# A two-layer decoder trunk with gathered expert rows: six row buffers and eleven held chunks in place of seven and ten, pooling moved to VectorE

## The chip, the core and the metric

One core of one Trainium2 chip. The metric is the device time of one execution, in microseconds (us); the kernel before takes 1603.8 us (median of 3 runs, 1603.68 to 1604.42). All arithmetic is float32.

## What is computed

The input x is 256 tokens by 1024 channels; each of two layers does this to it:

```python
h = rmsnorm(x, g_mix)
p, q, k, v, gl = split(h @ w_in)             # 512, 512, 512, 512 and 2048 columns
a = (trailing_mean(p, windows 2/4/8/16 on 4 groups of 128 channels) - p) @ w_pool * pool_scale
b = causal_attention(q, k, v, 8 heads, ALiBi) @ w_attn_up
x = x + (sigmoid(gl[:, :1024]) * a + sigmoid(gl[:, 1024:]) * b) @ w_out
xt = rmsnorm(x, g_ffn)
# per token and head (8 heads): two 128-key score lists, top 16 of each, top 16 of the 256 sums,
# softmax -> 16 experts out of 16384, each one row u of w_peer_u and one row v of w_peer_v
x = x + sum_over_128_experts(prob * gelu(u . xt) * v)
```

and a last rmsnorm ends it. With 256 tokens the attention is plain causal attention.

## The kernel before, in words

**Windows.** The work is cut into four windows (w = 0 to 3): layer 0 tile 0, layer 0 tile 1, layer 1 tile 0, layer 1 tile 1; a tile is 128 tokens, one on each partition. A window has a *stream* and a *mix*. The stream gathers the 128 expert rows of each token of the tile: gather g (0 to 511) is one indirect DMA from GpSimd's queue (line 1182) that brings, for each of 128 tokens, one u row and one v row, 8 KB per partition and 1 MB in all, into one of RING = 7 ring buffers. The mix is all that precedes it for the tile: norm, projections, attention, pooling, gates, the two output projections, and the queries and key searches that give the experts.

**Ticks.** The stream of a window runs over 64 ticks of two rows (r = 0 and 1). Except for window 0, whose mix runs first, the mix of window w runs inside the stream of window w - 1. Each engine's program is written out by `streamed` (line 311): the rows in order, and the pieces of the mixes between them wherever a generator's `yield when(w, tick)` says. `when` adds `TICKS * (w - 1) + MIX_START`, so with MIX_START = 4 a piece at 31 stands in tick 35 of the window before. Waits on an engine hold up all that stands behind them on it.

**One row.** VectorE multiplies the u half by the token and sums (`dot`, line 1051); ScalarE makes the gelu weight of it in five small operations (lines 789 to 797). Then the v half is added with that weight: on TensorE, after ScalarE writes the weight on a diagonal (line 807), by products with the diagonal that pile up in two PSUM banks, `ybank` (line 622, four instructions per row); or on VectorE straight into x (`weighted`, line 1064, one instruction, at the start of the next tick). `takes_chunk` (line 282) holds the ticks at which a weight chunk is due, and there row r = 0 goes to VectorE and only r = 1 to TensorE. GpSimd issues gather g when row g - 7 was added (it waits on pe_summed or dve_summed); it issues in order.

**Boundary of windows.** In `hand_over` (line 1037) VectorE writes the new tile's tokens with the gain that TensorE spread over the partitions (`everywhere`, line 352, at tick 58 of the mix); `close` (line 1067) waits until both engines have added all rows of the old window and adds ybank to x (line 1072), and TensorE waits for that before its first row of the new window (line 612). In the last window TensorE first loads x into ybank (line 616).

**Weights.** The weights of a layer are 30 chunks of 1 MB (w_in 0 to 15, attention up 16 and 17, w_out 18 to 21, queries 22 to 29), due at CHUNK_TICKS. Chunks 16 to 25 are *held* in SBUF for both tiles of a layer (HELD = 10), so the second tile does not load them again; the others pass through W_SLOTS = 2 slots, each refilled when its chunk was used. In window 0 the first 16 chunks pass through RING - 1 ring buffers, as the ring is idle then. SyncE's queue issues all chunk loads in order (line 1207), with `heads` (line 1209), which reloads keys and gains for layer 1 once the last query score of window 1's mix is computed.

**Pooling.** p comes out with tokens on partitions (`rows_by`, line 405) and is multiplied on TensorE by banded 128 x 128 matrices from `constants` (lines 496 to 514); for tile 0 a further product gives `carry`, what its last 16 tokens add to tile 1. ScalarE copies carry and the result mT to SBUF (lines 712 and 713).

## Time and profile before

| | |
|---|---|
| median of 3 runs | 1603.8 us |
| the profiled execution | 1599.52 us, span 1597.7 us |
| TensorE matmul busy | 84% of the span |
| VectorE, ScalarE, GpSimd busy | 69%, 58%, 41% |
| moved by DMA | 647.49 MB, mean 405 GB/s |
| row gathers | 512 of 1 MB |
| chunk loads | 100 of 1 MB (64 to the slots, 20 to held buffers, 16 to the ring) |
| granted TensorE clock, mean | 0.952 |

Busy shares are averages over the whole span. In the profile PE is TensorE, PEld its weight load, DVE VectorE, ACT ScalarE, POOL GpSimd and SP SyncE.

### The profile page before, as it was taken

How to read it: one execution, taken by the hardware profiler on the slowest of the kernel's cores; microseconds unless marked ns; L12 is line 12 of the kernel's file. 1: busy time of each engine (PE TensorE's matmuls, PEld its weight loads, DVE VectorE, ACT ScalarE, POOL GpSimd, SP SyncE). 2: the span in 40 equal slices, each digit the busy share in tenths (PEclk: the TensorE clock that was granted, in tenths of full speed). 3: DMA queues.
4: the chain of work that ended last, by engine and by line, in shares of the span. 5: the costliest groups of instructions: out<-in, count | busy, mean ns of one | idle time of the engine just before them, and what ended most of it. 6: DMA issues, size and time to landing. Idle time of an engine off the chain costs nothing.

```text
span 1597.7 us, 18942 instructions
## 1 busy us (share of the span) xinstructions
PE 1346.7 (84%) x5676; PEld 814.6 (51%) x5676; DVE 1097.2 (69%) x2608; ACT 932.2 (58%) x3344; POOL 655.5 (41%) x516
## 2 busy tenths in 40 slices
PE   8998888988987888977898887888988987777876
PEld 7985656644663356643465445655555522223222
DVE  1059978865777877745577797876667876777545
ACT  1226547557756645534775574555676666667766
POOL 0014434355444533323544353334444455455563
PEclk9999999999999999987999899989999999999999
DMA  9939999999999999999999999999999999999996
GB/s 381 391 125 423 422 423 422 424 419 398 413 421 418 410 422 423 422 425 421 392 420 422 392 419 424 423 422 423 397 407 423 421 422 421 421 421 419 415 422 283
DMA packets 90943, 647.49 MB, mean 405 GB/s; under 512 B 10024, under 2 KB 11480, under 8 KB 12504
## 3 DMA queue, kind: packets, MB, share of 16 engines
q0 software_dynamic: 73728, 536.90, 81.3%
q1 hardware_dynamic: 16788, 109.15, 16.5%
q8 instruction: 45, 0.74, 0.2%
q14 instruction: 58, 0.48, 0.1%
q10 hardware_dynamic: 324, 0.23, 0.0%
HBM read 645.19 MB, written 1.05 MB: 404 GB/s over the span
## 4 chain that ended last, share of the span: by engine, by line
DMA 47%; PE 25%; DVE 18%; issue 4%; ACT 4%; POOL 1%; DVEq 0%; ACTq 0%; POOLq 0%
DMA ring<-in_uv,expert 47%; PE ybank L622 12%; DVE ring L1051 7%; PE bank L433 6%; PE bank L571 4%; DVE xs L1064 2%; ACT wgt L797 1%; POOL ring L1182 1%; ACT diag L807 1%; PE bank L413 1%; DVE buf L836 1%; DVE si L842 1%; ACT th L795 1%; DVE ci L842 1%; DVE buf L886 1%
## 5 line engine op out<-in xcount | busy, mean ns | idle before, releaser
L1182 POOL DMA_INDIRECT ring<-in_uv,expert x512 | 655.3, 1280 | 921.6 <-PE ybank L622 584.6
L622 PE MATMUL ybank<-ring,diag 128*128 128x512 f32 x1664 | 836.3, 638 | 214.3 <-ACT diag L807 209.0
L1051 DVE SCALAR_TENSOR_TENSOR ring<-ring,tok 128x1024 f32<-128x1024 f32 x512 | 626.1, 1225 | 379.0 <-DMA ring<-in_uv,expert 373.9
L622 PEld LDWEIGHTS ybank<-ring,diag 128*128 128x128 f32 x1664 | 303.9, 197 | 650.5 <-ACT diag L807 388.9
L789 ACT ACTIVATE sq<-dots 128x1 f32<-128x1 f32 x512 | 103.1, 201 | 521.1 <-DVE ring L1051 520.5
L433 PEld LDWEIGHTS bank<-hT,wring 128*128 128x128 f32 x1664 | 199.0, 198 | 30.0 <-issue 23.5
L433 PE MATMUL bank<-hT,wring 128*128 128x128 f32 x1664 | 201.6, 281 | 8.9 <-DMA wring<-in_chunks 7.4
L797 ACT ACTIVATE wgt<-th,half_p 128x1 f32<-128x1 f32 x512 | 198.1, 387 | 17.1
L807 ACT ACTIVATE diag<-cst,wgt 128x128 f32<-128x128 f32 x416 | 167.0, 402 | 13.4
L795 ACT ACTIVATE th<-arg,dots 128x1 f32<-128x1 f32 x512 | 150.8, 295 | 16.6
L792 ACT ACTIVATE arg<-sq,gelu_bias 128x1 f32<-128x1 f32 x512 | 142.9, 279 | 0.0
L790 ACT ACTIVATE half_p<-dots,prob 128x1 f32<-128x1 f32 x512 | 142.8, 279 | 0.0
L1064 DVE SCALAR_TENSOR_TENSOR xs<-ring,wgt,xs 128x1024 f32<-128x1024 f32 x94 | 120.4, 1281 | 3.0 <-ACT wgt L797 1.8
L433 PEld LDWEIGHTS bank<-hT,held 128*128 128x128 f32 x480 | 58.5, 201 | 2.8 <-issue 2.8
L571 PE MATMUL bank<-held,buf 128*128 128x256 f32 x256 | 59.5, 388 | 0.0
L433 PE MATMUL bank<-hT,held 128*128 128x128 f32 x480 | 59.1, 284 | 0.0
L571 PEld LDWEIGHTS bank<-held,buf 128*128 128x128 f32 x256 | 50.2, 197 | 14.0 <-issue 7.4
L413 PE MATMUL bank<-wring,hT 128*128 128x256 f32 x192 | 47.3, 402 | 7.5 <-DMA wring<-in_chunks 7.5
L413 PEld LDWEIGHTS bank<-wring,hT 128*128 128x128 f32 x192 | 38.7, 204 | 22.4 <-issue 12.3
L633 ACT ACTIVATE buf<-bank 128x256 f32<-128x256 f32 (+2 forms) x67 | 29.5, 448 | 32.2 <-PE bank L433 30.6
L433 PE MATMUL bank<-hT,ring 128*128 128x128 f32 x384 | 45.6, 282 | 2.2 <-DVE hT L938 2.2
L433 PEld LDWEIGHTS bank<-hT,ring 128*128 128x128 f32 x384 | 45.1, 198 | 2.7 <-issue 2.6
(117 smaller groups left out, 843.6 us busy)
## 6 DMA issues: line engine op xcount, KB each, us to landing
wring<-in_chunks SPq DMA_DIRECT2D x64, 1024.0 KB, 9.7
held<-in_chunks SPq DMA_DIRECT2D x20, 1024.0 KB, 23.6
ring<-in_chunks SPq DMA_DIRECT2D x16, 1024.0 KB, 8.8
ring<-in_uv,expert POOLq DMA_INDIRECT x512, 12.0
xs<-in_x SPq DMA_DIRECT2D x2, 512.0 KB, 12.1
wpool<-in_w_pool SPq DMA_DIRECT2D x2, 512.0 KB, 15.1
trunk_out<-buf SPq DMA_DIRECT2D x4, 256.0 KB, 4.7
ring<-in_pool_scale SPq DMA_DIRECT2D x1, 512.0 KB, 11.5
```

What stands on the lines that cost most here:

```text
L433: ins = pe.matmul(b[:, m * CW + lo:m * CW + lo + P], wt[:, k, lo:lo + P], hT[:, k, :], start=(k == 0), stop=(k == KC - 1))
L571: ins = pe.matmul(b[:, 0:CW], mergedT[:, k, :], wt[:, k, :], start=(k == 0), stop=(k == KC - 1))
L622: ins = pe.matmul(ybank[m][:, :], diag[:, nth % DIAGS, :], ring[:, (2 * t + r) % RING, D + m * BANK:D + (m + 1) * BANK], start=(nth == ten ...
L789: act_stepped(act.activation(sq[:, r:r + 1], dots[:, c:c + 1], ACT.Square))
L790: act.activation(half_p[:, c:c + 1], dots[:, c:c + 1], ACT.Copy, scale=prob[:, 2 * n + r:2 * n + r + 1])
L792: act_stepped(act.activation(arg[:, r:r + 1], sq[:, r:r + 1], ACT.Identity, scale=0.044715 * GELU_C, bias=gelu_bias[:, 0:1]))
L795: act_stepped(act.activation(th[:, r:r + 1], arg[:, r:r + 1], ACT.Tanh, scale=dots[:, c:c + 1]))
L797: ins = act.activation(wgt[:, c:c + 1], th[:, r:r + 1], ACT.Identity, scale=half_p[:, c:c + 1], bias=half_p[:, c:c + 1])
L807: act.activation(diag[:, nth % DIAGS, :], ident, ACT.Copy, scale=wgt[:, c:c + 1]).then_inc(diag_done, 1)
L1051: dve.scalar_tensor_tensor(out=ring[:, g % RING, 0:D], in0=ring[:, g % RING, 0:D], scalar=1.0, in1=tok[:, :], op0=ALU.mult, op1=ALU.mult, ...
L1064: dve.scalar_tensor_tensor(out=total, in0=ring[:, (2 * t + r) % RING, D:2 * D], scalar=wgt[:, c:c + 1], in1=total, op0=ALU.mult, op1=ALU.a ...
L1182: pool.indirect_dma_start(ring[:, g % RING, :], None, uv, bass.IndirectOffsetOnAxis(ap=expert[:, at:at + 1], axis=0)).then_inc(row_landed[ ...
```

## The change

The same sums are computed; six things are edited.

1. RING 7 to 6, HELD 10 to 11 (chunk 26, a query chunk, is held too).
2. MIX_START 4 to 3; the due ticks of w_out and query chunks are further apart; the pieces that follow them (turns of x, their copies, key searches) move with them, and the last window's heads have a table of their own.
3. More rows go to VectorE: `shared` has, beside the chunk ticks, ticks 29 to 45 of each mix (EASY) and the first tick of windows 1 to 3.
4. The gain is spread behind query chunk 5 instead of at tick 58 of the mix.
5. Pooling: p is computed with channels on partitions (`cols_by`), ScalarE copies it beside the last 16 tokens of the tile before, and VectorE makes the trailing sums by four doubling additions, scales and subtracts. The banded matrices, their products and the copies of carry and mT go.
6. In the last window x is added to ybank at its 33rd tick, not loaded at its first.

```diff
-MIX_START = 4
-CHUNK_TICKS = (5, 6, 7, 8, 9, 10, 12, 13, 14, 15, 17, 18, 20, 21, 23, 24, 25, 26, 31, 32, 33, 34,
-               41, 43, 45, 47, 49, 51, 53, 55)
+MIX_START = 3
+CHUNK_TICKS = (5, 6, 7, 8, 9, 10, 12, 13, 14, 15, 17, 18, 20, 21, 23, 24, 25, 26, 31, 32.5, 34, 35.5,
+               42, 45, 48, 51, 54, 57, 60, 63)
+EASY = range(29, 46)
-HELD = 10
+HELD = 11
-RING = 7
+RING = 6
...
-        qT = sb("qT", [P, NA, P])
-        oT = mT = qT
-        p_sb = qT[:, :, :].rearrange("p a n -> p (a n)")
+        mix = sb("mix", [P, NG * (REACH + P)])
+        qT = oT = mix[:, 0:NA * P].rearrange("p (a n) -> p a n", n=P)
+        reached = mix[:, :].rearrange("p (g n) -> p g n", n=REACH + P)
+        mT = reached[:, :, 0:P]
...
+        later_heads = (46.5, 52, 57, 63, 68.5, 74, 79, 84)
+        last_heads = (46.5, 52, 63, 70, 77, 84, 91, 98)
...
-            return when(w, 46 + (15 if w == windows - 1 else 11) * h // 2 + 2 * step)
-        takes_chunk = {when(w, n) for w in range(1, windows) for n in CHUNK_TICKS} | set(first_queries)
+            return when(w, (last_heads if w == windows - 1 else later_heads)[h] + 2 * step)
+        shared = {when(w, ceil(n)) for w in range(1, windows) for n in (*CHUNK_TICKS, *EASY)} | set(first_queries)
+        shared |= {TICKS * w for w in range(1, windows)}
...
-            return (1,) if t in takes_chunk else (0, 1)
+            return (1,) if t in shared else (0, 1)
...
-            yield from rows_by(C_P, "p", a_done)
+            yield from cols_by(C_P, "p", 2, v_done)
             yield from cols_by(C_GATE, "gate0", 2)
             yield when(w, 16)
...
-            b = claim("m", a_done)
-            for g in range(NG):
-                mine, lo, first = p_sb[:, g * P:(g + 1) * P], C_OWN + g * P, C_FIRST + g * REACH
...
-            filled("m", ins)
...
-            yield when(w, 37)
+            yield when(w, 36.5)
             if w:
                 turn_mixed(0)
+            yield when(w, 38)
             turn_mixed(1)
+            yield when(w, 39.5)
             turn_mixed(2)
...
-                if w == 0 and h == 1:
-                    pe.wait_ge(gains_in, 16)
+                if h == (PH - 3 if w else 1):
+                    pe.wait_ge(gains_in, 16 * (layer + 1))
                     everywhere(pe, w, G_FFN, "gain")
...
-            if w:
-                yield when(w, 58)
-                everywhere(pe, w, G_FFN, "gain")
...
-            if last and n == r == 0:
+            if last and n == TICKS // 2 and r == 0:
                 pe.wait_ge(x_mixed, OUTS * windows)
+                pe.wait_ge(dve_summed, vector_rows(t))
                 for m in range(2):
-                    pe.matmul(ybank[m][:, :], ident, x_of(w % NT)[:, m * BANK:(m + 1) * BANK], start=True, stop=False)
+                    pe.matmul(ybank[m][:, :], ident, x_of(w % NT)[:, m * BANK:(m + 1) * BANK], start=False, stop=False)
...
             yield when(w, 15)
-            copy_out("p", p_sb, flat)
+            if w % NT:
+                act.wait_ge(*read(w - 1, "p"))
+                act.activation(reached[:, :, 0:REACH], carried, ACT.Copy)
+            act.activation(reached[:, :, REACH:], blocks(filled_bank(act, w, "p")), ACT.Copy).then_inc(p_copied, 1)
...
-                act.activation(carry[:, :], filled_bank(act, w, "carry")[:, 0:NG * REACH], ACT.Copy).then_inc(a_done, 1)
-            copy_out("m", mT[:, :, :])
...
             dve.reciprocal(srec[:, :], ssum[:, :]).then_inc(srec_done, 1)
+            dve.wait_ge(p_copied, w + 1)
+            if tile == 0:
+                step(dve.tensor_copy(carried, reached[:, :, P:]))
+                step(dve.memset(reached[:, :, 0:REACH], 0.0))
+                settle(dve)
+            for g in range(NG):
+                n = REACH + P - 2 * 2 ** g + 1
+                step(dve.tensor_tensor(reached[:, g:, 0:n], reached[:, g:, 0:n], reached[:, g:, 2 ** g:n + 2 ** g],
+                                       ALU.add))
+                settle(dve)
+            yield when(w, 16.5)
+            if tile == 0:
+                for g, wide in enumerate(WINDOWS):
+                    lo = REACH - wide + 1
+                    step(dve.tensor_tensor(reached[:, g, lo:lo + REACH], reached[:, g, lo:lo + REACH],
+                                           cst[:, C_SHORT + g * REACH:C_SHORT + (g + 1) * REACH], ALU.mult))
+                settle(dve)
+            b = bank("p")
+            for g, wide in enumerate(WINDOWS):
+                lo = REACH - wide + 1
+                ins = dve.scalar_tensor_tensor(out=mT[:, g, :], in0=reached[:, g, lo:lo + P], scalar=1.0 / wide,
+                                               in1=b[:, g * P:(g + 1) * P], op0=ALU.mult, op1=ALU.subtract)
+            ins.then_inc(v_done, 1)
...
-                yield when(w, 33 + n)
+                yield when(w, 33 + 1.5 * n)
```

The table of constants shrinks by 576 columns of 128 x 4 bytes.

## Rows read from the trace of the kernel before

**Rows 1.** Page, DMA totals, and what each kind of chunk load moves.

```profile
DMA packets 90943, 647.49 MB, mean 405 GB/s; under 512 B 10024, under 2 KB 11480, under 8 KB 12504
...
wring<-in_chunks SPq DMA_DIRECT2D x64, 1024.0 KB, 9.7
held<-in_chunks SPq DMA_DIRECT2D x20, 1024.0 KB, 23.6
```

**Rows 2.** Stretches of 20 us: PE, PEld, DVE, ACT, POOL busy, clock, DMA share, GB/s.

```profile
80.00:100.00 20.00, 19.70 (x117) 17.52 (x116) 5.83 (x12) 2.39 (x8) 0.00 (x0) 1.00 0.17 69
240.00:260.00 20.00, 17.61 (x94) 12.69 (x95) 19.35 (x57) 15.51 (x59) 8.28 (x6) 0.91 1.01 421
360.00:380.00 20.00, 20.00 (x64) 11.79 (x63) 11.05 (x20) 12.96 (x48) 9.30 (x8) 1.00 0.98 375
760.00:780.00 20.00, 20.00 (x69) 12.19 (x68) 11.59 (x19) 13.38 (x50) 10.67 (x10) 1.00 0.96 367
900.00:920.00 20.00, 16.80 (x32) 6.01 (x31) 16.75 (x44) 10.99 (x43) 7.51 (x7) 0.90 0.95 360
1140.00:1160.00 20.00, 20.00 (x61) 10.53 (x60) 9.92 (x17) 14.35 (x55) 9.75 (x9) 1.00 0.97 383
1180.00:1200.00 20.00, 20.00 (x101) 13.31 (x100) 14.01 (x35) 12.92 (x47) 8.13 (x9) 1.00 0.98 391
```

**Rows 3.** Timeline 1519 to 1524 us: two dots, each started by a landing.

```profile
1519.71 1.23 DVE L1051 SCALAR_TENSOR_TENSOR ring<-ring,tok 128x1024 f32<-128x1024 f32 x1 [1.26 <-DMA ring<-in_uv,expert]
...
1522.19 1.23 DVE L1051 SCALAR_TENSOR_TENSOR ring<-ring,tok 128x1024 f32<-128x1024 f32 x1 [1.24 <-DMA ring<-in_uv,expert]
```

**Rows 4.** Gathers (L1182) of 1490 to 1570 us: duration min/median/max in ns, then landing.

```profile
L1182 POOL DMA_INDIRECT ring<-in_uv,expert x32: 936/1672/1686, 1490.7 to 1568.2; - x32
...
DMA to landing us min/median/max: 11.6/12.0/13.0
```

**Rows 5.** Gathers of 892 to 912 us, across a window's boundary.

```profile
L1182 POOL DMA_INDIRECT ring<-in_uv,expert x5: 936/936/936, 896.1 to 910.9; - x5
...
DMA to landing us min/median/max: 5.5/6.4/11.1
```

**Rows 6.** Gathers of 210 to 245 us, where VectorE is fullest.

```profile
L1182 POOL DMA_INDIRECT ring<-in_uv,expert x8: 936/977/1677, 211.8 to 244.3; - x8
...
DMA to landing us min/median/max: 11.5/15.0/19.0
```

**Rows 7.** Chain that ended last: start, us, what.

```profile
354.29 1.72 PE ybank L622 x4
356.00 3.45 PE bank L571 x16
...
369.80 10.30 PE ybank L622 x24
...
410.92 3.57 PE bank L433 x32
...
895.87 3.71 PE bank L358 x16
...
905.54 1.28 DVE xs L1072 x2
```

**Rows 8.** Timeline of window 0's mix, TensorE, and the first gather.

```profile
47.94 0.96 PE L500 MATMUL bank<-cst,qT 128*128 128x16 f32 x8
...
50.61 7.32 PE L433 MATMUL bank<-hT,ring 128*128 128x128 f32 x64
...
108.16 1.07 POOL L1182 DMA_INDIRECT ring<-in_uv,expert  x1 [107.71 <-DVE expert L897]
```

**Rows 9.** VectorE's groups: busy us, mean ns of one, then idle before.

```profile
L1064 DVE SCALAR_TENSOR_TENSOR xs<-ring,wgt,xs 128x1024 f32<-128x1024 f32 x94 | 120.4, 1281 | 3.0 <-ACT wgt L797 1.8 <-issue 0.2 <-DVE wpool L971 0.2
...
L886 DVE TENSOR_TENSOR buf<-buf,sif 128x256 f32<-128x256 f32 (+2 forms) x66 | 27.4, 416 | 2.3
...
L994 DVE TENSOR_TENSOR buf<-buf 128x512 f32<-128x512 f32 x8 | 5.5, 693 | 0.8
```

More of the change, by code:

```diff
@@ L9 @@
 from contextlib import ExitStack
+from math import ceil
 import numpy as np
@@ L73 @@
 OUTS = 4
+REACH = max(WINDOWS)
 C_ID = 0
@@ L98, in constants @@
     q, k = np.arange(P)[:, None] + (NT - 1) * P, np.arange(S)[None, :]
-    c[:, C_DIST:C_OWN] = np.where(k <= q, k - q, MASKED)
+    c[:, C_DIST:C_SHORT] = np.where(k <= q, k - q, MASKED)
     for g, w in enumerate(WINDOWS):
-        for tile in range(NT):
-            t, src = np.arange(P) + tile * P, np.arange(S)[:, None]
-            inside = (src <= t) & (src > t - w)
-            m = np.where(inside, 1.0 / np.minimum(t + 1, w), 0.0) - (src == t)
-            lo, n = (C_OWN + g * P, P) if tile else (C_FIRST + g * REACH, REACH)
-            c[:, lo:lo + n] = m[tile * P:(tile + 1) * P, 0:n]
-        lo = C_BEFORE + g * REACH
-        c[:, lo:lo + REACH] = m[0:P, 0:REACH]
+        c[:, C_SHORT + g * REACH:C_SHORT + (g + 1) * REACH] = w / np.minimum(np.arange(REACH) + 1, w)
     return c
@@ L488, in tensor_mix @@
                 filled(f"qk{n}", ins)
-            yield from rows_by(C_P, "p", a_done)
+            yield from cols_by(C_P, "p", 2, v_done)
             yield from cols_by(C_GATE, "gate0", 2)
             yield when(w, 16)
-            pe.wait_ge(*read(w, "p"))
-            if w == 0:
-                pe.wait_ge(tables_in, 16)
-            if tile == 0:
-                b = claim("carry", a_done)
-                for g in range(NG):
-                    lo = C_BEFORE + g * REACH
-                    ins = pe.matmul(b[:, g * REACH:(g + 1) * REACH], p_sb[:, g * P:(g + 1) * P], cst[:, lo:lo + REACH],
-                                    start=True, stop=True)
-                filled("carry", ins)
-            b = claim("m", a_done)
-            for g in range(NG):
-                mine, lo, first = p_sb[:, g * P:(g + 1) * P], C_OWN + g * P, C_FIRST + g * REACH
-                if tile == 0:
-                    pe.matmul(b[:, g * P:g * P + REACH], mine, cst[:, first:first + REACH], start=True, stop=True)
-                    ins = pe.matmul(b[:, g * P + REACH:(g + 1) * P], mine, cst[:, lo + REACH:lo + P],
-                                    start=True, stop=True)
-                else:
-                    pe.matmul(b[:, g * P:(g + 1) * P], mine, cst[:, lo:lo + P], start=True, stop=False)
-                    ins = pe.matmul(b[:, g * P:g * P + REACH], ident, carry[:, g * REACH:(g + 1) * REACH],
-                                    start=False, stop=True)
-            filled("m", ins)
             if tile == 0 and layer:
@@ L623, in tensor_row @@
                                 ring[:, (2 * t + r) % RING, D + m * BANK:D + (m + 1) * BANK],
-                                start=(nth == tensor_rows(w * TICKS) and not last),
+                                start=(nth == tensor_rows(w * TICKS)),
                                 stop=(nth == tensor_rows((w + 1) * TICKS) - 1))
```

27 lines of the change are left out of this document (13 added, 14 removed).

## The prediction

> **What bounds the kernel now.** First the bytes. The page counts 647.49 MB, with slot and held chunks of 1024 KB each [rows 1]; by 20 us stretches the DMA engines move 421 GB/s at a share of 1.01 even where VectorE is busy 19.35 of 20 us, at 240 to 260 [rows 2]. 647.49 MB at 423 GB/s are 1531 us of a span of 1597.7: nearly all of the kernel is transfer, so what counts is what removes bytes or what lets the queue run dry, and no engine's busy share. The stretches show where that happens. From 80 to 100 us the share is 0.17: the weights of window 0 are in, and the gathers wait for its mix. Later five stretches dip, to 375, 367, 360, 383 and 391 GB/s [rows 2]. In four of them TensorE is busy 20.00 of 20; the fifth, 900 to 920, is the boundary of windows 1 and 2.
>
> Next the ring. Undisturbed, landings follow each other by 2.48 us [rows 3], and a gather lands 12.0 us after its issue [rows 4]. A buffer comes round in 7 x 2.48 = 17.4 us, so between landing and the next issue lie 17.4 - 12.0 = 5.4 us: dot, weight, diagonal, sum. A short queue shows as a short way to landing. At the boundary it falls to 5.5 us [rows 5], which I take as the bare time of a gather with nothing ahead of it. Seven buffers therefore bear 17.4 - 5.5 = 11.9 us from landing to reissue, six bear 14.9 - 5.5 = 9.4 us. That margin is what the change spends. Eight stretches of the whole run have a gather that landed in under 8.4 us, in windows 0 to 2 and their boundaries; rows 5 show the worst.
>
> Last the chain, for durations: a row costs TensorE 1.72 us, a w_out chunk 3.45, a query chunk 3.57, the spread gain 3.71; behind the four w_out chunks of a mix six rows wait in a pile of 10.30 us [rows 7].
>
> **The change part by part**, against the profiled execution of 1599.5 us.
>
> *Bytes.* Chunk 26 is not loaded for windows 1 and 3: 2 x 2.48 = 5.0 us less in windows 0 and 2, where the queue is full. The table of constants loses 0.29 MB, but it loads before 80 us, and the queue then has nothing to do until the first gather at 108.16 us [rows 2, 8]: nothing. Between nothing (if the queue goes dry by as much) and 5.0 I take **-5.0**.
>
> *Window 0's mix.* TensorE is on the chain there. The products for carry and mT run from 47.94 to 50.61 [rows 8] and go; p by columns costs about the same two chunks. All behind it, to the first gather, comes 2.7 us earlier, and the DMA is idle in front of that gather. The new pooling block stands on VectorE, idle in this stage, while TensorE does two gate chunks of 3.66 us each (7.32 [rows 8]): hidden; without that cover it would cost up to 4 us. With five chunk buffers in the ring in place of six a chunk is asked for one use later, and has four chunk times, 14.3 us, to land: hidden, at least while it lands as the slots' do, in 9.7 us [rows 1]. **-2.6**, bounds -2.7 and +1.4.
>
> *Output and first query stage.* Every tick from 32 to 48 of windows 0 to 2 now gives TensorE one row, and w_out chunks come each 1.5 ticks: 3.45 + 1.5 x 1.72 = 6.0 us of 7.4, where it was 3.45 + 1.72 = 5.2 of 5.0. The pile of six rows does not form. Query chunks each three ticks leave it 3.57 + 5 x 1.72 = 12.2 of 14.9. What do the four dips give back? By bytes they lack (423 - 375 + 423 - 367 + 423 - 383 + 423 - 391) / 423 x 20 = 8.3 us; by the share that is missing from 1.01 only 3.0 us. The second is nearer to what the queue lost, as engines that ran ahead also move fewer bytes; I take **-4.6**. The price is 11 more rows per window on VectorE, 1.28 us each [rows 9], at ticks without key searches: two dots of 1.23 [rows 3] and one sum are 3.7 us of 5.0. It is free there as VectorE has nine of 20 us idle, at 360 to 380 [rows 2], and worth up to 42 us if it had none.
>
> *Pooling in the stream.* VectorE gets four additions of 572, 423, 274 and 129 elements. Between 416 ns for 256 and 693 ns for 512 elements [rows 9] they are near 0.75, 0.60, 0.44 and 0.29 us; with four subtractions of 128 that is 3.1 us for tile 1, and 4.0 us for tile 0 with its copies and small products. It stands at ticks 19 to 20, in the stage where VectorE is fullest. There a gather still takes 11.5 us to land [rows 6], thanks to chunk loads between rows, 6.0 above the bare time; the lost buffer takes some 3.7 of that and the block 3.1. One window goes dry by about 1 us: **+1.0**, bounds 0 and 10.2 (all three blocks on the path). The pool products of TensorE stand 3.5 ticks later, so they do not wait.
>
> *Sixth buffer at the boundaries.* With the ticks moved, query chunks 5, 6 and 7 fall on ticks 60, 63 and 66 and the gain goes behind chunk 5. TensorE then has 10 rows, three chunks, the gain and three scores (four products of the chunk's 3.57 / 32 each) in seven ticks: 17.2 + 10.7 + 3.7 + 1.3 = 32.9 of 34.7 us, with a solid block of 3.57 + 3.71 = 7.3 at tick 60. Landing to reissue is then 5.4 + 7.3 = 12.7 us where 9.4 are borne, 3.3 too many, less what row 0 on VectorE and the chunk loaded at that tick (2.48 us more time) give back. On the other side tick 64w no longer puts a row of TensorE behind the closing sums of 1.28 us [rows 7]. `heads` moves from tick 61 to 68 with score 7, and with it, behind it on SyncE's queue, the first chunks of layer 1, due at tick 8 of window 1 (four ticks, 20 us, for a landing of 9.7: in time); but no chunk fills the queue at that boundary. I take 1.5, 2.0 and 1.0 us for the three boundaries: **+4.5**, bounds 0 and 7.4 (each dry by a whole slot).
>
> *The rest.* ScalarE loses 36 diagonals and gains one small copy, beside idle time. The add of x to ybank at tick 32 of the last window is the same four products.
>
> **Sum:** -5.0 - 2.6 - 4.6 + 1.0 + 4.5 = -6.7 us. The profiled execution would be 1592.8; it stood 4.3 us (0.27%) under the median, so the forecast for the median is 1603.8 - 6.7 = **1597.1 us**.
>
> **A rule weighed.** The bare time of 5.5 us comes from rows 5. The Trainium skill, in "DMA: Bandwidth & Descriptors", section on the anatomy of one software-generated DMA, fits 2.0 us + bytes / 436 GB/s, which would be 4.4 us for 1 MB, an estimate by that page. By it six buffers would bear 10.5 us and the boundary term would be some 3 us smaller, 1594; the row decides, as it includes 0.94 us of issue.
>
> **The rivals.**
> *A, only bytes and start pay.* The old dips go, but new shallow ones come at each of the 24 query chunks, as 5.4 + 3.57 + 0.45 for a score = 9.4 us is just what six buffers bear: 0.2 too many each is 4.8 us more. 1597.1 + 4.8 = 1602, no change that can be told. For it speaks that in the query stage even seven buffers came down to under 8.4 us; against it that row 0 of that tick is on VectorE, and that three ticks instead of two lie between chunks.
> *B, slower: the query stage starves.* When VectorE is late by one search piece (three instructions of 0.42 us, 1.25 in all [rows 9]) at the same tick as a query chunk, landing to reissue is 10.7 us, 1.3 too many. At 12 of 24 chunks that is 16 us, and the old dips are not recovered: -5.0 - 2.6 + 16 = +8.4, **1612 us**. It decides once the mean loss per query chunk passes 0.32 us (7.6 / 24). For it: the eight short stretches; with six buffers each starts 2.48 us lower. Against it: most chunks now have nothing else on TensorE for three ticks.
> *C, the issue is slowed.* A gather's issue takes 936 ns where VectorE pauses [rows 5] and 1672 ns where the dot runs beside it [rows 4]. Each row moved to VectorE, and each addition, can put 0.74 us more on an issue. A dry ring loses that once per round of six rows; with 48 rows in short stretches this is 8 x 0.74 = 6 us: 1603. This is a rule of the Trainium skill too: "GPSIMD Engine Reference", Specifications, says that GpSimd's SBUF interface is shared with VectorE's instructions of two SBUF inputs; by that rule, the trace agrees, 0.94 against 1.67 us. Against it: where the queue is 9 us deep the issue is hidden.
>
> **How the numbers follow.** Forecast's case 0.57, A 0.16, B 0.19, C 0.08. Low end: dips worth 8.3 and neither new term, -15.9 us: 1588. High end: B less its last part, 1611. A measurement here tells about 0.2%, 3.2 us, from no change. Faster by more than that: the forecast's case, 0.57, almost whole, with a little of A and C for its own slower part, 0.58; slower: B and the worst of C, 0.21; within: 0.21.
>
> **What would show it.** Right: 645.1 MB on the page; the first gather near 105.5 us; quiet gathers landing in 9.5 us, at unchanged 2.48 us spacing; no pile of TensorE rows behind w_out; 130 sums on VectorE in place of 94; short landings (5.5 to 6) at ticks 60 to 66. Wrong: dips under 400 GB/s in the query stages (B), a landing to reissue over 9.4 us at ticks 18 to 24 (pooling mis-sized), or a DMA share below 1.0 in the last window, where six buffers should be enough.

## The result, and the profile after

The changed kernel takes 1625.49 us (median of 4 runs, 1620.2 to 1629.04) where the kernel before takes 1603.74 on the same chip (4 runs, 1603.09 to 1604.42): a ratio of 1.0133 [1.0121, 1.0145]. It is slower by 21.8 us; 1597.1 was forecast, and 1611 was the upper end. The profiled execution is the slowest of the four, 1629.04 us with a span of 1627.2.

The page of the kernel after answers rows 1 and 9:

```profile
PE 1296.0 (80%) x5580; PEld 795.6 (49%) x5580; DVE 1151.5 (71%) x2688; ACT 915.2 (56%) x3304; POOL 662.0 (41%) x516
...
DMA packets 90654, 645.08 MB, mean 396 GB/s; under 512 B 9992, under 2 KB 11576, under 8 KB 12472
...
L1189 POOL DMA_INDIRECT ring<-in_uv,expert x512 | 661.8, 1293 | 947.3 <-PE ybank L604 528.7
L604 PE MATMUL ybank<-ring,diag 128*128 128x512 f32 x1520 | 791.8, 655 | 293.1 <-ACT diag L790 290.5
L1058 DVE SCALAR_TENSOR_TENSOR ring<-ring,tok 128x1024 f32<-128x1024 f32 x512 | 624.7, 1224 | 350.8 <-DMA ring<-in_uv,expert 344.9
...
L1071 DVE SCALAR_TENSOR_TENSOR xs<-ring,wgt,xs 128x1024 f32<-128x1024 f32 x130 | 166.6, 1282 | 12.1 <-ACT wgt L780 10.7
```

What the edit was to remove is gone: 2.4 MB fewer, 130 sums on VectorE at the old 1.28 us each. But the mean rate fell from 405 to 396 GB/s, and that outweighs the bytes: 645.08 MB at 396 GB/s are 1629 us. Fewer bytes, moved with more pauses. The stretches say where (columns as in rows 2):

```profile
80.00:100.00 20.00, 19.70 (x117) 17.51 (x116) 4.63 (x10) 2.76 (x10) 0.00 (x0) 1.00 0.53 223
120.00:140.00 20.00, 16.02 (x74) 10.80 (x74) 14.07 (x41) 10.04 (x37) 4.77 (x5) 0.89 0.59 217
...
360.00:380.00 20.00, 16.38 (x59) 10.28 (x57) 14.52 (x21) 10.97 (x41) 10.73 (x10) 1.00 0.99 394
440.00:460.00 20.00, 18.84 (x92) 12.99 (x92) 17.40 (x49) 12.83 (x48) 7.27 (x8) 0.95 0.94 359
500.00:520.00 20.00, 12.68 (x45) 7.72 (x45) 18.19 (x40) 10.97 (x43) 7.32 (x5) 0.75 0.91 359
...
760.00:780.00 20.00, 17.41 (x60) 11.75 (x59) 14.87 (x22) 11.11 (x43) 12.15 (x8) 0.91 1.02 422
...
1180.00:1200.00 20.00, 14.29 (x26) 6.02 (x27) 14.29 (x22) 13.04 (x50) 10.02 (x8) 0.68 1.01 417
1240.00:1260.00 20.00, 17.02 (x65) 9.96 (x64) 17.58 (x50) 12.23 (x44) 9.46 (x8) 0.91 0.91 354
```

The dips of [rows 2] under the w_out chunks did shrink: 360 to 380 rose from 375 to 394, 760 to 780 from 367 to 422, and TensorE is no longer busy 20.00 of 20. New dips stand elsewhere, with the share itself down to 0.91 to 0.94: in the last ticks of a window (440 to 460, 1240 to 1260) and in its first (500 to 520), and one of 0.59 behind the first gathers (120 to 140), most of which is no cost of the change, as shown in the last section.

How a dip comes about is seen in one row. The timeline of the kernel after, ticks 61 to 63 of window 0's stream:

```profile
486.46 1.67 POOL L1189 DMA_INDIRECT ring<-in_uv,expert  x1 [1.25 <-DVE xs L1071]
486.82 3.73 PE L437 MATMUL bank<-hT,wring 128*128 128x128 f32 x32
...
488.72 0.40 ACT L790 ACTIVATE diag<-cst,wgt 128x128 f32<-128x128 f32 x1
489.11 1.22 DVE L1058 SCALAR_TENSOR_TENSOR ring<-ring,tok 128x1024 f32<-128x1024 f32 x1 [1.78 <-DMA ring<-in_uv,expert]
...
490.49 2.05 PE L362 MATMUL bank<-gains,cst 24*128 24x128 f32 x16
...
492.46 5.85 PE L604 MATMUL ybank<-ring,diag 128*128 128x512 f32 x13
...
495.22 1.08 POOL L1189 DMA_INDIRECT ring<-in_uv,expert  x1 [5.85 <-PE ybank L604]
```

A diagonal is ready at 489.12 and waits behind query chunk 5 and the gain until 492.46, so GpSimd, idle for 5.85 us, reissues that buffer at 495.22 (the 13 products of 492.46 are those of several rows, up to the end of the view). Its row had landed at 484.5, 10.7 us earlier (landings of this kernel are the events of the six buffers' semaphores in the trace). Meanwhile VectorE already sits idle 1.78 us for a landing. This is the block of the prediction, at its place but shorter: 5.6 us (486.82 to 492.46) for 7.3. The prediction took 3.71 us for the gain from one instance [rows 7]; here its sixteen products take 2.05. That instance had run at a granted clock of 0.50, the lower of the two levels (1.2 GHz), as the kernel before shows around it (columns as in rows 2):

```profile
895.00:900.00 5.00, 5.00 (x19) 3.98 (x18) 4.18 (x13) 2.01 (x7) 0.94 (x1) 0.50 1.01 418
```

At its other places behind the first gather the kernel before spreads the gain in 2.05 us too. Of the 10.7 us of this row the block is 3.3 us of waiting; another 1.6 us passed before VectorE, busy with a key search and a sum, began the dot at 486.10.

### The profile page after: what moved, and what is told of

Its sections match the earlier page's. It is cut to its first block, busy times and chain, and to the rows that moved or that the text cites. A ratio compares the mean times of both kernels' runs of the same rounds, so it can differ in the third digit from the quotient of the medians.

```text
span 1627.2 us, 18779 instructions
## 1 busy us (share of the span) xinstructions
PE 1296.0 (80%) x5580; PEld 795.6 (49%) x5580; DVE 1151.5 (71%) x2688; ACT 915.2 (56%) x3304; POOL 662.0 (41%) x516
## 2 busy tenths in 40 slices
DMA packets 90654, 645.08 MB, mean 396 GB/s; under 512 B 9992, under 2 KB 11576, under 8 KB 12472
## 4 chain that ended last, share of the span: by engine, by line
DMA 43%; PE 27%; DVE 17%; ACT 7%; issue 5%; POOL 1%; another core or an unknown queue 0%; DVEq 0%; ACTq 0%; POOLq 0%
DMA ring<-in_uv,expert 40%; PE ybank L604 13%; PE bank L437 8%; DVE ring L1058 7%; DMA wring<-in_chunks 3%; PE bank L553 2%; DVE xs L1071 2%; ACT diag L790 1%; ACT wgt L780 1%; POOL ring L1189 1%; ACT th L778 1%; PE bank L417 1%; DVE si L825 1%; ACT sq L772 1%; ACT arg L775 1%
## 5 line engine op out<-in xcount | busy, mean ns | idle before, releaser
L1189 POOL DMA_INDIRECT ring<-in_uv,expert x512 | 661.8, 1293 | 947.3 <-PE ybank L604 528.7
L604 PE MATMUL ybank<-ring,diag 128*128 128x512 f32 x1520 | 791.8, 655 | 293.1 <-ACT diag L790 290.5
L1058 DVE SCALAR_TENSOR_TENSOR ring<-ring,tok 128x1024 f32<-128x1024 f32 x512 | 624.7, 1224 | 350.8 <-DMA ring<-in_uv,expert 344.9
L604 PEld LDWEIGHTS ybank<-ring,diag 128*128 128x128 f32 x1520 | 281.1, 201 | 691.8 <-ACT diag L790 448.8
L437 PEld LDWEIGHTS bank<-hT,wring 128*128 128x128 f32 x1728 | 210.6, 200 | 39.2 <-issue 26.9
L437 PE MATMUL bank<-hT,wring 128*128 128x128 f32 x1728 | 211.5, 283 | 11.4 <-DMA wring<-in_chunks 11.4
L1071 DVE SCALAR_TENSOR_TENSOR xs<-ring,wgt,xs 128x1024 f32<-128x1024 f32 x130 | 166.6, 1282 | 12.1 <-ACT wgt L780 10.7
L790 ACT ACTIVATE diag<-cst,wgt 128x128 f32<-128x128 f32 x380 | 152.6, 402 | 12.3
L437 PEld LDWEIGHTS bank<-hT,held 128*128 128x128 f32 x608 | 79.0, 210 | 12.6 <-issue 12.6
L437 PE MATMUL bank<-hT,held 128*128 128x128 f32 x608 | 77.8, 291 | 0.0
L1058 DVE DVE_READ_ACCUMULATOR ring<-ring,tok 128x1 f32 x512 | 42.0, 82 | 0.0
L825 DVE FIND_INDEX8 si<-sv,buf 128x8 uint32<-128x128 f32 x128 | 34.9, 285 | 0.0
## 6 DMA issues: line engine op xcount, KB each, us to landing
xs<-in_x SPq DMA_DIRECT2D x2, 512.0 KB, 11.9
```

What stands on the lines that cost most here:

```text
L437: ins = pe.matmul(b[:, m * CW + lo:m * CW + lo + P], wt[:, k, lo:lo + P], hT[:, k, :], start=(k == 0), stop=(k == KC - 1))
L604: ins = pe.matmul(ybank[m][:, :], diag[:, nth % DIAGS, :], ring[:, (2 * t + r) % RING, D + m * BANK:D + (m + 1) * BANK], start=(nth == ten ...
L790: act.activation(diag[:, nth % DIAGS, :], ident, ACT.Copy, scale=wgt[:, c:c + 1]).then_inc(diag_done, 1)
L1058: dve.scalar_tensor_tensor(out=ring[:, g % RING, 0:D], in0=ring[:, g % RING, 0:D], scalar=1.0, in1=tok[:, :], op0=ALU.mult, op1=ALU.mult, ...
L1071: dve.scalar_tensor_tensor(out=total, in0=ring[:, (2 * t + r) % RING, D:2 * D], scalar=wgt[:, c:c + 1], in1=total, op0=ALU.mult, op1=ALU.a ...
L1189: pool.indirect_dma_start(ring[:, g % RING, :], None, uv, bass.IndirectOffsetOnAxis(ap=expert[:, at:at + 1], axis=0)).then_inc(row_landed[ ...
```

## The experiments

Ratios are compared, not microseconds, since the runs came from more than one chip: the kernel before took 1603.3 and 1603.7 us in the first two sets and 1596.7 to 1598.1 in the later ones. Two theories stood at the start: R, the sixth buffer costs the time; S, the order of work or the additions do. For the tables by stage I read the start of each dot (L1051 before, L1058 after) and subtract that of the same row in a second kernel.

### Which part of the change costs it

`e1_six_alone` is the kernel before with these two lines:

```diff
-HELD = 10
+HELD = 11
-RING = 7
+RING = 6
```

> The kernel before with RING = 6 and HELD = 11 and nothing else. Theory R (the sixth buffer costs what was lost; the new schedule and the pooling give time back): with the old schedule the loss is larger than the whole change's 21.7 us, so 1630 to 1645 us. Theory S (the new schedule and the pooling cost it, the ring is nearly free as six buffers bear 9.4 us from landing to reissue): 1598 to 1608 us.

Measured: 1.0168 [1.0134, 1.0201], +27.7 us. `e2_seven_back` is the reverse, the changed kernel with seven and ten:

> The changed kernel with RING = 7 and HELD = 10 again. Theory R: the new schedule with seven buffers is faster than the kernel before, 1593 to 1600 us (the start 2.6 us earlier, old dips gone). Theory S: the loss stays without the 5 us of bytes, 1618 to 1632 us.

Measured: 0.9994 [0.9984, 1.0004], no difference. `e3_after_again` is the changed kernel once more:

> The changed kernel once more, as its runs spread over 1620.2 to 1629.0 us. If the stretch from 111.8 to 127 us of its profile, where ScalarE stands still for 3.5 us and the seventh gather goes out at 127.0 us, belongs to the program, the second profile shows it too, within 1 us. If it was that one execution, the seventh gather goes out before 122 us and the time of the profiled run is some 5 us less.

Measured: 1.0139 [1.0119, 1.0159]. Neither outcome was met as written: the seventh gather goes out at 124.87 us, but the first went out 1.35 us earlier too, and the pause before the seventh is 12.22 us against 13.05. The stretch is there again; whether it belongs to the program is taken up in the last section. `e4_pool_alone` is the kernel before with the pooling block on VectorE and nothing else:

> The kernel before with the pooling on VectorE and nothing else. By the prediction's terms: -2.6 us at the start and nothing in the stream with seven buffers, 1600 to 1603 us, first gather near 105.6 us. If the pooling block on VectorE is what costs (theory P), 1606 to 1615 us.

Measured: 0.998 [0.997, 0.9989]. So in the order of before the ring costs more than the whole loss, 27.7 us; the pooling gives 3 to 4; and the rest of the new order takes some 2 us of that back (0.9994 with it, 0.998 without). Theory S falls. R holds for the ring, but not for the 1593 to 1600 us that it expected of the new order with seven buffers (1602.7). From the changed kernel down to its seven-buffer partner it is 1.0136 (the mean of its two timings) less 0.9994, 23 us. The parts add up: -3.5 for the pooling, +2 for the order, +23 for the ring are 21.5 of the 21.8 us.

`e6_six_ten` (RING = 6, HELD = 10) and `e5_eight_nine` (RING = 8, HELD = 9) take the two sizes apart:

> The kernel before with six row buffers and ten held chunks, so the ring alone at the same bytes. The kernel with six and eleven took 1631.0 us; both theories V and Q expect the missing bytes to be worth little where the queue runs dry anyway: 1631 to 1637 us. Were the eleventh held chunk itself the cost (its load comes in one piece with the others of its layer), this one would be near 1604.

> The kernel before with eight row buffers and nine held chunks: one buffer more and 2 MB more of loads (5.0 us by the bytes). Theory V (the buffers bear what VectorE is late by in the first ticks of a window, where key searches and chunk loads meet) has a steep loss from seven to six that flattens with more buffers: the eighth gives back the few short stretches that seven left, 4 to 10 us, against 5.0 us of bytes: 1597 to 1604 us. Theory Q (the queue needs its depth everywhere; every row pays for a buffer less) has the loss go on evenly: the eighth buffer gives some 20 us less 5.0 of bytes, 1585 to 1590 us.

Measured: 1.017 [1.0153, 1.0187], +27.6 us, for six and ten; 1.0008 [0.9998, 1.0017], +1.1 us, for eight and nine. Six buffers with ten or with eleven held chunks take the same time: the 2 MB that the eleventh saves are worth nothing once the queue runs dry. The eighth buffer makes up about 3.9 of 5.0 us of bytes, if those bytes cost their full price; no run has eight buffers with ten chunks, so 3.9 is the most that it gives, give or take 1.5 by the interval. Seven is the knee: one fewer costs 27.6 us, one more gives at most some 4. Theory Q of the expectations (each buffer is worth the same) falls.

### Where it is lost

Each column is a kernel with six buffers less its partner with seven on the same chip, start of the dot at each tick, us: the changed kernel (first profile, then `e3_after_again`) less `e2_seven_back`; with query chunks halved, `e13_split` less `e15_split_seven` (which also loads the first chunks of layer 1 earlier); with short searches, `e9_short_after` less `e10_short_back`. These kernels are explained below. The chip of the first profile is not on record; its kernel before took 1603.7 us, that of e2 1603.3.

```
window, tick     after   after again   halved   short searches
0, 0              +0.4      -0.9        -0.5        +0.8
0, 16             +6.2      +3.8        +4.5        +4.8
0, 48             +6.3      +2.8        +5.2        +2.6
1, 0             +11.3      +7.1        +6.2        +9.0
1, 16            +16.9     +11.9        +8.7       +11.5
1, 48            +16.8     +12.9       +10.9       +12.2
2, 0             +22.2     +16.6        +9.9       +15.6
2, 16            +26.1     +21.3       +10.3       +16.6
2, 48            +25.1     +19.1       +12.6       +18.0
3, 0             +26.7     +20.6       +10.3       +20.5
3, 16            +28.3     +24.0       +14.3       +24.4
3, 63            +29.2     +23.5       +14.1       +24.7
```

In the first column 16.9 us are lost in ticks 0 to 16 of the four windows, 12.0 in the three stages from tick 48 to the next window's 0, and nothing in between; in the second 17.6 and 9.5. (The first is the slowest execution of its kernel against the fastest of e2, so its total is above the 23 us of the ratios.) In ticks 0 to 16 VectorE does the last key searches of the tile while the next mix begins; from 48 on the query chunks come. With the chunks halved nothing is lost from 48 on (-2.3), and 11.9 us remain in ticks 0 to 16. With short searches it is 11.4 in ticks 0 to 16, and 12.3 from 48 on.

### Short searches

VectorE's part is tested by doing less of it, with both rings:

```diff
+n = 16 if lo else data(0).shape[1]
-if lo:
-    for r in each:
-        step(dve.match_replace(data(r), vals(r)[:, 0:8], data(r), LOWEST))
-    settle(dve)
...
-step(dve.max(vals(r)[:, lo:lo + 8], data(r)))
+step(dve.max(vals(r)[:, lo:lo + 8], data(r)[:, 0:n]))
```

(max_index likewise.) Before's order with seven and with six buffers (ten held):

> The kernel before (seven buffers, ten held chunks), but the second eight of every key search and sum search is taken from the first 16 columns alone, and the eight already found are not struck out. The experts are others than the reference's; gathers, bytes, rows and every other step stay. VectorE has some 5 to 6 us less to do per head. Theory V: before's few short stretches go as well, 1590 to 1600 us. Theory Q: no difference by more than the 3 us of an earlier first gather, 1599 to 1604 us.

> The same shortened searches with six buffers and ten held chunks. Theory V: the cost of the sixth buffer falls from the some 30 us between the full kernels to under 12 us between this and its seven-buffer partner, 1600 to 1610 us, and gathers land after 8 us or more in ticks 4 to 16 of windows 1 and 2. Theory Q: the gap stays at 20 us or more, 1620 us or over.

Measured: 0.9991 [0.9982, 1.0001] with seven and 1.0189 [1.0151, 1.0226] with six, a spread of 1623 to 1642 us. Theory V, that VectorE's searches are what the seventh buffer bears, falls in this order: the gap stays, 29 us by the medians (1630.98 and 1602.1 us) and 32 by the ratios, as theory Q had it here. In the changed order:

> The changed kernel (six buffers, eleven held) with the shortened searches: the second eight of every key search and sum search is taken from the first 16 columns alone, the eight already found are not struck out, and so the experts are others; gathers and bytes stay. In the order of before, short searches took away what six buffers lost in the first 16 ticks of windows 0 to 2, and left what they lost in the query stages (some 20 us of 28). Theory M (six buffers lose wherever landing to reissue passes 9.4 us: by late VectorE in the search ticks, by query chunks and the gain in the query stage; the changed order has mended the second place and not the first) now expects nearly all of the loss of the changed kernel to go: 1595 to 1606 us, and under 3 us lost between rows at ticks 0 and 16 of windows 1 and 2. Theory Q (queue depth costs everywhere): 1618 us or more.

> Partner of the run before: the changed kernel with seven buffers and ten held chunks, with shortened searches. Its full searches took 1602.7 us. Theory M: 1592 to 1600 us, within 8 us of the one before (which has 5 us fewer bytes). Theory Q: 20 us or more below the one before.

Measured: 1.01 [1.0083, 1.0117] and 0.9978 [0.9968, 0.9988]. Short searches make the changed kernel some 6 us faster (1.0136 to 1.0100), but its seven-buffer partner some 3 us faster too (0.9994 to 0.9978), so the gap between them only falls from 23 to 20 us (0.0122), and the intervals do not tell 3 us from nothing. Theory M had expected nearly all of the loss to go, and falls as stated; the gap is the 20 us that theory Q had named. The reading that the expectation starts from (short searches took away the loss of the first 16 ticks in the order of before) came from the profile of `e8_short_six`, the fastest of its four executions by 5 us.

The profile pairs gathers with landings in these two kernels. In the last window, 1490 to 1570 us, six buffers; then seven buffers, same stretch; and around the boundary of windows 1 and 2 (840 to 890), six buffers:

```profile
L1186 POOL DMA_INDIRECT ring<-in_uv,expert x31: 939/1666/1863, 1491.8 to 1567.2; - x31
...
DMA to landing us min/median/max: 6.4/9.6/10.6
```
```profile
DMA to landing us min/median/max: 11.0/12.0/12.0
```
```profile
DMA to landing us min/median/max: 6.1/8.8/12.2
```

Undisturbed, a gather lands 9.6 us after its issue with six and 12.0 with seven [rows 4]: one slot of 2.48 us less in hand, as forecast, and at full rate.

### Halved blocks

TensorE's part is tested by halving its blocks, with VectorE untouched:

```diff
 for half in range(2):
+    if half and w and c >= C_PQ:
+        yield due(c + m) + 0.5
...
-everywhere(pe, w, G_FFN, "gain")
+for n in range(2):
+    if w:
+        yield query_tick(w, h) + 1 + n / 2
+    everywhere(pe, w, G_FFN, "gain", (n,))
```

> The changed kernel (six buffers, full searches) with each query chunk of windows 1 to 3 given to TensorE in two halves, one row of TensorE between them, and the gain in two halves a row apart. No block on TensorE in the query stage is then longer than 1.9 us. Against its seven-buffer partner the changed kernel loses 23 us, 12 of them between ticks 48 of one window and 0 of the next. Theory B (the blocks that TensorE works off between a landing and the reissue are that part): 8 to 12 us come back, ratio to before 1.0135 - 0.006 = 1.006 to 1.0085. Rival W (there too VectorE is late; the blocks are only beside it): under 3 us, ratio 1.012 to 1.014.

Measured: 1.0079 [1.0051, 1.0106]; from 1.0136 that is 9 us back, give or take 5 by the intervals, as theory B had it; the rival's under 3 us is outside. The timeline of `e13_split` at the place shown above:

```profile
481.46 1.95 PE L439 MATMUL bank<-hT,wring 128*128 128x128 f32 x16
...
485.63 1.95 PE L439 MATMUL bank<-hT,wring 128*128 128x128 f32 x16
...
486.57 1.14 POOL L1194 DMA_INDIRECT ring<-in_uv,expert  x1 [1.69 <-PE ybank L609]
...
487.42 1.88 PE L609 MATMUL ybank<-ring,diag 128*128 128x512 f32 x4
...
489.23 1.15 PE L362 MATMUL bank<-gains,cst 24*128 24x128 f32 x8
489.57 0.94 POOL L1194 DMA_INDIRECT ring<-in_uv,expert  x1 [1.86 <-PE ybank L609]
```

No block is longer than 2 us, GpSimd's idle time falls from 5.85 to 1.69 and 1.86 us, and the same row is reissued 7.4 us after its landing (479.2 to 486.6) in place of 10.7. Over ticks 40 to 63 of the windows, 18 rows of the changed kernel pass 9.4 us from landing to reissue (the longest 13.1 us, tick 61 of window 1), and 2 of this one.

> The same halves and the shortened searches of VectorE (experts are others than the reference's). Shortened searches alone had the changed kernel at a ratio of 1.0100. If two causes share the loss (TensorE's blocks in the query stage, VectorE's searches at the start of a window) and each alone leaves the other, both together leave under 8 us of difference to the seven-buffer kernel with short searches (ratio 0.9978): 0.998 to 1.003. If the gap is a matter of queue depth alone: 1.008 or more.

Measured: 1.0047 [1.0032, 1.0061]. Both together bring back 14 us, some 3 of which short searches give with seven buffers too, and 0.0069 (11 us) to the seven-buffer kernel with short searches remain, above the 8 that were expected. So of the gap of 23 us the halves take away 9, which is shown, and the searches 3 on top, which is within the noise of the times and shown only by stage in the profiles: one cause found, one likely, and a rest. `e16_split_all` halves the column chunks at the start of a window too:

> The changed kernel (six buffers) with all chunks of w_in that come by columns, and not the query chunks alone, in two halves a row of TensorE apart. Theory B: the blocks at the start of a window (ticks 5 to 10 of the mix, one chunk per tick) are part of the loss of the search ticks: some 3 to 5 us beyond e13_split. Rival (VectorE alone sets the pace there): the same as e13_split within 2 us.

Measured: 1.0086 [1.007, 1.0103], the same as e13_split within the intervals: no gain from the single chunks at the start of a window, though one of the 3 us that theory B named can't be excluded (the difference is +1 us, give or take 5).

### With seven buffers, is anything left?

`e11_loads_first` is e2_seven_back with `c == 0` replaced by `c == 2` in the condition that calls `heads`; `e15_split_seven` adds the halves:

> The changed kernel with seven buffers and ten held chunks, and one line of SyncE's program changed: the first two weight chunks of layer 1 are issued ahead of the wait for window 1's last score, not behind it. In the kernel without this line the gain of 5 to 7 us at a boundary was given back by tick 8 of the next window. Theory L (at the boundary of windows 1 and 2 it was given back because the chunk loads stood behind that wait and met the search ticks): 3 to 6 us gained over 1602.7, 1597 to 1600 us. Rival (the gathers only reach the same full search ticks earlier, where VectorE sets the pace): no difference, 1601 to 1604 us.

> The changed kernel with seven buffers and ten held chunks, the first chunk loads of layer 1 ahead of the wait for the last score (ratio 0.9991), and the halves as in the run before. Theory B: seven buffers bear 11.9 us, so the blocks cost little: ratio 0.996 to 0.999. Rival W: no change, 0.9985 to 1.000.

Measured: 0.9991 [0.9981, 1.0001] and 0.9989 [0.9979, 0.9998]: the order of the loads and the blocks cost nothing with seven that these runs can tell (0.9989 lies in the ranges of both theories). `e12_pool_easy` is e4_pool_alone with `EASY = range(29, 46)`:

> The kernel before with the pooling on VectorE (1599.2 us) and the rows r = 0 of ticks 29 to 45 of each mix on VectorE as well, everything else as before: seven buffers, ten held. By the prediction's term of the output stage the dips there give back up to 4.6 us: 1594 to 1597 us. Rival: those dips are refilled later by bytes that have to move anyway only where the queue is short, or the rows are hidden by seven buffers: 1598 to 1600 us.

Measured: 0.999 [0.9981, 1.0], no better than e4's 0.998. The stretch 360 to 380, first in e4_pool_alone, then in e12_pool_easy:

```profile
360.00:380.00 20.00, 20.00 (x72) 13.35 (x71) 13.01 (x22) 12.87 (x48) 8.39 (x7) 1.00 0.98 396
```
```profile
360.00:380.00 20.00, 15.07 (x49) 8.64 (x47) 15.47 (x23) 11.79 (x46) 11.75 (x8) 0.91 1.01 419
```

The dip of 396 GB/s is mended, to 419, and the time does not show it. A dip in GB/s whose share is 0.98 was hardly a loss.

The last two, with 11 executions each, are e4_pool_alone with the query chunks halved, and e4_pool_alone as it was:

> The kernel before with the pooling on VectorE (ratio 0.998) and the query chunks of windows 1 to 3 in two halves, seven buffers, ten held. In the kernel before, the landings that fall short of the bare time and one slot add up to 7.1 us, most of it at query chunks (ticks 42 and 49). If the halves take these away: 0.9955 to 0.997. If seven buffers bear them anyway, as in e15_split_seven: 0.9975 to 0.9985.

> e4_pool_alone again, with more rounds: the pooling on VectorE alone, seven buffers. By its first timing 0.997 to 0.999; a ratio whose interval holds 1 would say that the first timing was chance.

Measured: 0.9979 [0.997, 0.9988] and 0.9978 [0.9969, 0.9987]. The kernel before with the pooling moved, and nothing else of the change, beats both kernels: 3.5 us under before.

## Why the prediction was wrong

**The step that failed is "Sixth buffer at the boundaries", +4.5 with bounds 0 and 7.4.** Its mechanism was right: short landings mean a dry queue, and chunk 5 with the gain makes a block behind which a buffer waits. Its size was not: the sixth buffer costs 23 us against the seven-buffer partner. From tick 48 to the next window the profiled changed kernels lose 12.0 and 9.5 us, and in ticks 0 to 16 of the windows, on which the prediction put nothing beyond the boundaries, 16.9 and 17.6. It was not that the block was taken too short: it is 5.6 us and not 7.3, as said above. Two errors are in it.

*The tally.* I counted the stretches in which a gather landed in under 8.4 us, found eight, and priced three boundaries. A buffer less takes one slot of 2.48 us from every gather. So every stretch of before that lands in under 5.5 + 2 x 2.48 = 10.5 us falls short with six, by 10.5 minus its shortest landing. From the same trace that sum is 49.1 us, in 24 stretches of consecutive gathers, 19 of them at ticks 40 to 63 (the first four ticks of window 0, where the ring only fills, left out). It was there to be read. As gathers behind a late one make some of it up, I read it as an upper bound: the ring cost 27.6 us, 0.56 of it. The same tally of the other runs (10.5 where a buffer is to be taken away, 8.0 where not):

```
                                     shortfall, us   measured
before, to lose one buffer (10.5)       49.1         +27.6 (six and ten)
changed order, seven, to lose one       47.2         +23
short searches, before's, to lose one   43.2         +29 to +32
short searches, changed, to lose one    40.7         +20
halves, seven, to lose one              32.8         +14
before, to gain one (8.0)                7.1          -3.9 at most (eight; 5.0 of bytes taken off)
before with six buffers (8.0)           31.8         +27.6
changed kernel (8.0)                    28.4         +23 over its seven-buffer partner
changed, query chunks halved (8.0)      21.4         +14 over e15_split_seven
```

In all five pairs that lose a buffer the time lies below the sum, at 0.43 to 0.74 of it. The tally of one profile is rough: `e4_pool_alone` and `e18_pool_again` are the same kernel, and give 54.9 and 40.7 us at 10.5, and 7.2 and 1.4 at 8.0. So the row for gaining a buffer says little.

*The margin.* 9.4 us from landing to reissue was used as a sharp limit, with 5.4 us as what a row needs ahead of a block. In before's trace 52 rows pass 9.4 us, 36 of them in ticks 0 to 27. Most of those cost nothing: outside the first four ticks of window 0 only 9 gathers of before land in under 8.0 us. I take it that a chunk load fills the queue in that time; no run tests that. The landing time, which holds both, is the reading to go by.

*The start* looked like a third. "Window 0's mix", -2.6, was right up to the first gather: 106.71 us here and 105.4 in e3_after_again, for 108.16 [rows 8]. Just behind it the seventh gather waits (first three lines after; the last one is the eighth gather of before):

```profile
113.05 0.94 POOL L1189 DMA_INDIRECT ring<-in_uv,expert  x1 [0.30 <-issue]
116.77 5.78 PE L437 MATMUL bank<-hT,held 128*128 128x128 f32 x32
127.04 1.68 POOL L1189 DMA_INDIRECT ring<-in_uv,expert  x1 [13.05 <-DVE xs L1071]
```
```profile
122.36 1.68 POOL L1182 DMA_INDIRECT ring<-in_uv,expert  x1 [5.19 <-DVE xs L1064]
```

GpSimd issues nothing for 13.05 us (12.22 in e3_after_again), and the share falls to 0.59. But a pause of 10.6 to 12.5 us stands there in e2, e4 and e7 with seven buffers too, and of 10.7 in e5 with eight, and in e9_short_after, e13, e14 and e16 with six it is only 6.3 to 6.9, against 5.2 with seven. So the sixth buffer lengthens this pause by one to two us, and the rest comes and goes from one execution to another (last section).

**Point by point:**

- *Bytes, -5.0:* wrong here. Held 10 or 11 with six buffers is 1.0170 against 1.0168. The lower bound "nothing (if the queue goes dry by as much)" was the case.
- *Output and first query stage, -4.6:* wrong. The dips are mended and the pile of six rows is gone, as forecast, and e12_pool_easy, which has the rows on VectorE but the old due ticks, shows that with seven buffers it is worth nothing. Of the two readings, missing bytes (8.3 us) and missing share (3.0), neither was; the share was nearer.
- *Pooling in the stream, +1.0:* nothing is lost to the seven-buffer partner in ticks 16 to 48, where it stands (in the table by stage +0.1, -0.1 and -1.0 us, in the second profile -1.0, +1.0 and -2.2), though no run has the changed kernel without it. Its price was right: 3.8 us on VectorE in window 0's mix for 4.0 forecast (three of its five groups below, without the copy and the fill, 0.25 us; the last line is what stands behind it), and 3.5 us gained in all by e18_pool_again.

```profile
44.75 2.20 DVE L951 TENSOR_TENSOR mix<-mix 128x572 f32<-128x572 f32 x4
46.98 0.43 DVE L958 TENSOR_TENSOR mix<-mix,cst 128x16 f32<-128x16 f32 x4
47.45 0.88 DVE L964 SCALAR_TENSOR_TENSOR mix<-mix,bank 128x128 f32<-128x128 f32 x4
48.24 1.22 DVE L973 TENSOR_TENSOR wpool<-wpool,ring 128x1024 f32<-128x1024 f32 x1
```

- *The rule weighed:* by the fit in the Trainium skill's "DMA: Bandwidth & Descriptors", section on the anatomy of one software-generated DMA, a bare gather would take 4.4 us, an estimate, and six buffers would bear more. The shortest landings are 5.5 us in before [rows 5], 5.3 in the changed kernel and 5.0 in e1_six_alone; the row was nearer, and the rule would have made the forecast worse.
- *Rivals:* B (slower, "the query stage starves") is the nearest: it named the query chunks, and their halves brought back 9 us. Its price of 1612 was too low, since it left out the first ticks of a window, and its chance of 0.19 too small. A's shallow dips at query chunks are real as well: I wrote that 9.4 us "is just what six buffers bear" and took 0.2 us each, where the row shown above needed 10.7. C, slower issues, falls by the pages: the mean issue takes 1293 ns in the changed kernel, 1280 in before, and 1320 with seven buffers, which took 23 us less:

```profile
L1189 POOL DMA_INDIRECT ring<-in_uv,expert x512 | 675.8, 1320 | 901.6 <-PE ybank L604 542.6
```

**What stays open:** about 11 us of the loss with six buffers, which neither halves nor short searches bring back. Some 4 of them fall in ticks 0 to 16 of window 0 (e14_split_short against e10_short_back, two chips, neither with the wait of the last section: -0.6 at tick 0, +3.9 at tick 16), 4 between tick 48 and the end of that window, and 3.5 in ticks 0 to 16 of window 3. And why the changed order gains nothing with seven buffers, although its gathers start 2 us earlier, was not taken apart. In its trace 28 rows pass the 11.9 us that seven buffers bear, all in ticks 0 to 27, where before has 6; but e4_pool_alone, which is faster, has 20, so that is not the answer by itself.

## What to carry to other kernels

Before taking a buffer from a queue, list the time from issue to landing of every transfer, not of the worst few: each stretch under the bare time plus two slots is lost in part, and in the five pairs here the price was half to three quarters of the sum, and never above it. The price of depth has a knee (here 27.6 us for the seventh buffer, at most 4 for the eighth), so the seventh's price says nothing of the eighth's. When a buffer short of the knee is all there is, halve the longest blocks on the engine between landing and reissue before anything else; and do not count bytes saved where the queue runs dry, nor a dip in GB/s whose share is near 1.

## What the runs showed of the hardware that was not expected

The spread of the executions is wider with the short ring: 2.3 to 5.0 us for the kernels with seven or eight buffers (10 or 11 executions each), 4.4 to 18.3 with six (4 to 7 each). The widest is six buffers with short searches (1623.4 to 1641.8, with its seven-buffer partner at 5.0 on the same chip), but six and ten has 4.4 only.

The other thing is a wait that stands in some executions and not in others, whatever the ring and the order. Behind the first gathers ScalarE sits idle for 3.5 to 6.5 us until something that the profile can't name ("remote"). It is in nine of the profiled executions (the first of the changed kernel and e1 to e8, with six, seven and eight buffers) and in none of the other eleven (before and e9 to e18). The same kernel shows both, first e4_pool_alone, then e18_pool_again:

```profile
115.49 0.38 ACT L614 ACTIVATE buf<-bank 128x256 f32<-128x256 f32 x1 [3.61 <-remote]
115.93 1.22 PE L577 MATMUL bank<-beside,buf 128*128 128x128 f32 x4 [4.24 <-ACT buf L614]
116.94 5.84 PE L436 MATMUL bank<-hT,held 128*128 128x128 f32 x32
127.27 1.68 POOL L1187 DMA_INDIRECT ring<-in_uv,expert  x1 [11.48 <-DVE xs L1069]
```
```profile
111.83 0.36 ACT L614 ACTIVATE buf<-bank 128x256 f32<-128x256 f32 x1
112.79 3.74 PE L436 MATMUL bank<-hT,held 128*128 128x128 f32 x32
121.02 1.68 POOL L1187 DMA_INDIRECT ring<-in_uv,expert  x1 [5.18 <-DVE xs L1069]
```

TensorE stands idle behind it for 3.5 to 5.6 us where it is 0.5 otherwise, and then its clock is granted near the lower of its two levels (1.2 GHz) for part of the next stretch, so that the 32 products of a query chunk take 5.4 to 6.2 us in place of 3.74. The changed kernel, then the kernel before:

```profile
114.00:121.00 7.00, 5.25 (x24) 5.25 (x25) 4.04 (x12) 0.86 (x2) 0.00 (x0) 0.52 1.00 415
```
```profile
114.00:121.00 7.00, 4.58 (x39) 4.20 (x37) 5.66 (x15) 2.70 (x11) 2.56 (x3) 1.00 0.98 382
```

The gather that waits on this goes out 14.2 us after the first one where the wait is absent, and 19.5 to 21.4 where it is present; e4's profile is 4.2 us behind e18's at the last row. All profiles with the wait come from the two chips on which the kernel before took 1603.3 and 1603.7 us, or from the first run of the changed kernel, and those of the experiments without it from the three with 1596.7 to 1598.1. It may be what those chips differ by; no run shows that, and its cause stays open. A learner should take from it that one profile against one other can differ by 4 us in which the change has no part: look whether a wait stands in both.
